# Retention rope: rotating by a matmul instead of a stream shuffle, with moved weight splits and one bank less

## The reference

```
q = xpos_rotary(q, pos)
k = xpos_rotary(k, pos) * d ** -0.5

def rotate_every_two(x):
    x1, x2 = x[..., ::2], x[..., 1::2]
    return stack((-x2, x1), axis=-1).reshape(x.shape)

def xpos_rotary(x, pos):
    return x * cos(phase) + rotate_every_two(x) * sin(phase)
```

## Time and profile before

| what | value |
|---|---|
| median of 3 runs | 1906.66 us (1906.11 to 1907.75) |
| profiled execution | 1907.75 us, its span 1906.0 us |
| TensorE busy | 98% of the span |
| TensorE weight loads | 80% |
| VectorE busy | 64% |
| ScalarE busy | 42% |
| mean granted TensorE clock | 0.996 of full |
| DMA, mean | 84 GB/s |
| TensorE in the chain that ended last | 94% |

### The profile page before, as it was taken

One profiled execution on the slowest core, in us unless ns is written; L12 is line 12 of the kernel. 1 busy time (PEld: TensorE's weight loads), 2 busy tenths in 40 slices (PEclk: granted clock), 3 DMA queues, 4 the chain that ended last, 5 costly groups with the idle time before them and its releaser, 6 DMA issues.

```text
span 1906.0 us, 21837 instructions
## 1 busy us (share of the span) xinstructions
PE 1867.9 (98%) x8604; PEld 1517.2 (80%) x8604; DVE 1227.9 (64%) x1764; ACT 797.6 (42%) x1286; POOL 0.2 (0%) x4
## 2 busy tenths in 40 slices
PE   8999999999999999999999999999999899999999
PEld 6766889788888888766788888887888688888887
DVE  5865865667777434676767777336888667777521
ACT  4237411544444333355644444325665544444311
POOL 0000000000000000000000000000000000000000
PEclk9999999999999999999999999999999999999999
DMA  6211100232232233211333322322111033223232
GB/s 230 96 59 55 56 23 7 81 113 91 97 100 97 91 99 101 87 34 34 111 100 99 99 91 93 102 92 79 65 45 45 24 110 100 93 95 100 91 100 75
DMA packets 48646, 160.13 MB, mean 84 GB/s; under 512 B 5528, under 2 KB 6040, under 8 KB 48416
## 3 DMA queue, kind: packets, MB, share of 16 engines
q1 hardware_dynamic: 48544, 158.74, 25.6%
HBM read 156.62 MB, written 2.10 MB: 83 GB/s over the span
## 4 chain that ended last, share of the span: by engine, by line
PE 94%; ACT 3%; DVE 2%; issue 1%; DMA 0%; SPq 0%; ACTq 0%; DVEq 0%
PE bank L166 93%; DVE mixer_arena L1059 1%; ACT mixer_arena L647 1%; ACT wh L647 1%; PE bank L535 0%; DVE mixer_arena L1067 0%; ACT L647 0%; DVE wl L1059 0%; ACT conf_diag_l L647 0%; ACT conf_diag_h L647 0%; DMA raw<-in_w_in 0%; ACT even_arena L647 0%; DVE sq L1059 0%; PE bank L368 0%; DVE even_arena L1556 0%
## 5 line engine op out<-in xcount | busy, mean ns | idle before, releaser
L647 ACT ACTIVATE wh<-raw 128x1024 fp32r<-128x1024 f32 (+2 forms) x310 | 308.8, 998 | 735.4 <-PE bank L166 726.0
L166 PE MATMUL bank<-nh,wh 128*128 128x512 f32 x1520 | 600.5, 395 | 8.3 <-DVE nl L1067 8.3
L166 PE MATMUL bank<-nl,wh 128*128 128x512 f32 x1520 | 593.0, 390 | 0.0
L166 PE MATMUL bank<-nh,wl 128*128 128x512 f32 x1520 | 592.9, 390 | 0.0
L1059 DVE TENSOR_TENSOR wl<-raw,wh 128x1024 fp32r<-128x1024 f32 (+2 forms) x310 | 355.8, 1148 | 247.2 <-ACT wh L647 246.3
L166 PEld LDWEIGHTS bank<-nh,wh 128*128 128x128 f32 x1520 | 286.3, 188 | 74.4 <-DVE wl L1059 8.9
L166 PEld LDWEIGHTS bank<-nl,wh 128*128 128x128 f32 x1520 | 286.2, 188 | 61.1 <-issue 2.6
L166 PEld LDWEIGHTS bank<-nh,wl 128*128 128x128 f32 x1520 | 286.2, 188 | 60.1
L166 PE MATMUL bank<-ff_yh,wh 128*128 128x512 f32 x528 | 205.4, 389 | 0.0
L166 PE MATMUL bank<-ff_yl,wh 128*128 128x512 f32 x528 | 205.4, 389 | 0.0
L166 PE MATMUL bank<-ff_yh,wl 128*128 128x512 f32 x528 | 205.4, 389 | 0.0
(11 more groups left out here) (193 smaller groups left out, 1784.9 us busy)
## 6 DMA issues: line engine op xcount, KB each, us to landing
raw<-in_ff_a_up SPq DMA_DIRECT2D x44, 512.0 KB, 3.2
raw<-in_ff_b_up SPq DMA_DIRECT2D x44, 512.0 KB, 3.3
raw<-in_ff_c_up SPq DMA_DIRECT2D x44, 512.0 KB, 3.2
raw<-in_w_in SPq DMA_DIRECT2D x32, 512.0 KB, 3.3
raw<-in_pw SPq DMA_DIRECT2D x24, 512.0 KB, 3.3
raw<-in_even_in SPq DMA_DIRECT2D x16, 512.0 KB, 3.2
raw<-in_ff_a_down_a SPq DMA_DIRECT2D x8, 512.0 KB, 3.2
raw<-in_ff_a_down_b SPq DMA_DIRECT2D x8, 512.0 KB, 3.2
```

The source lines that it names most:

```text
L166: return e.matmul(out, lhsT, rhs, start=start, stop=stop, skip_group_check=True)
L647: return e.activation(out, in_, func, **kw).then_inc(n.give(sem), 1)
```

## The change

The neighbour swap of each rope becomes a f32 matmul with a constant 128x128 matrix `rotate` (entries 1 and -1, so the sin table loses its signs). `swap(s)` on TensorE writes bank 4 + s % 2, and VectorE's sin product reads that bank. The rotations stand behind pieces 3 to 7 (s = 0 to 4), behind piece 8 (s = 5 and 6) and behind the first token piece (s = 7). Rope 4 moves before the gates' scaling. A load for `rotate` goes between those of the tables and `select`. The GDN's piece i = 0 uses bank 0 instead of 6. VectorE scales the token blocks after the last `feed()` of the token pieces. The first `feed()` of the gate pieces moves on ScalarE behind the three silus, and on VectorE before the eight head scalings.

```diff
+    def swap(s):
+        e.wait_ge(c.evac, s + 1)
+        if s >= 2:
+            e.wait_ge(c.rope_done, s - 1)
+        x = (m1.rq if s < HEADS else m1.rk)[:, s % HEADS, :]
+        mm(bank[4 + s % 2][:, :], m1.rotate, x, True, True).then_inc(n.give(c.swap_done), 1)
...
             root_columns(6)
+            e.wait_ge(c.mix_ready, 16 * 3)
+        if s >= 3:
+            swap(s - 3)
     take(0)
     piece(0, c.nh, c.nl, range(DK))
-    e.wait_ge(c.mix_ready, 16 * 2)
-    token_pieces()
+    swap(5)
+    swap(6)
+    token_pieces(between={0: (7,)}, fn=swap)
...
     for i in range(12):
-        j = i % 2 if i else 6
-        take(j)
-        piece(j, c.nh, c.nl, range(DK))
+        take(i % 2)
+        piece(i % 2, c.nh, c.nl, range(DK))
...
         if i == 1:
-            vacate(6)
...
     roots_of(8, 4, 1.0)
-    feed()
     for q in (9, 10, 11):
         silu(q)
     for i in range(9):
         if i < 8:
-            if i:
-                feed()
+            feed()
             group()
...
     def rope(s):
         x = (m1.rq if s < HEADS else m1.rk)[:, s % HEADS, :]
         e.wait_ge(c.evac, s + 1)
-        settle()
-        e.stream_shuffle(m1.ropes[2 + s % 2], x, [i ^ 1 for i in range(32)]).then_inc(n.give(c.vec_step), 1)
         tt(m1.ropes[s % 2], x, m1.cos, ALU.mult, c.vec_step)
-        settle()
-        tt(m1.ropes[2 + s % 2], m1.ropes[2 + s % 2], m1.sin, ALU.mult, c.vec_step)
+        e.wait_ge(c.swap_done, s + 1)
+        tt(m1.ropes[2 + s % 2], bank[4 + s % 2][:, :], m1.sin, ALU.mult, c.vec_step)
         settle()
         tt(x, m1.ropes[s % 2], m1.ropes[2 + s % 2], ALU.add, c.rope_done)
...
         if s >= 4:
             rope(s - 4)
+    rope(4)
     z, az, ln = m1.z[0:64, :], m1.az[0:64, :], m1.ln[0:64, :]
     arrive()
     tt(z, bank[0][0:64, :], c.r[0:64, :], ALU.mult, c.evac)
     feed()
-    rope(4)
...
     for w in range(RING):
         arrive()
-        if w == RING - 1:
-            e.wait_ge(c.rcol_ready, 1)
-            for t in range(TB):
-                ts(m1.rv[:, t, :], bank[t][:, :], c.rcol[:, t:t + 1], ALU.mult, c.evac)
         feed()
...
+    e.wait_ge(c.rcol_ready, 1)
+    for t in range(TB):
+        ts(m1.rv[:, t, :], bank[t][:, :], c.rcol[:, t:t + 1], ALU.mult, c.evac)
...
-            if i == 0:
-                for q in range(4, 12):
-                    head_scale(q)
-                settle()
             feed()
+        if i == 0:
+            for q in range(4, 12):
+                head_scale(q)
+            settle()
...
             load(m1.tables, d["tables"], c.mix_ready)
+            load(m1.rotate, d["rotate"], c.mix_ready)
             load(m1.select, d["select"], c.mix_ready)
```

More of the change, by code:

```diff
@@ L118 @@
  tap_done conv_done silu_done glu_done ah_ready al_ready
- ea_ready gates_for_act gates_logged rope_done
+ ea_ready gates_for_act gates_logged swap_done rope_done
  ret_scored ret_weighed ret_done ret_copied decay_rows gcols_done gcols_ready spread spread_taken spread_used dec_ready decayed
@@ L1269, in vector_program @@
             e.wait_ge(c.gdn_conv, i - 2)
-        scaled(m1.pad[:, i % 3, TAPS_GDN - 1:TAPS_GDN - 1 + S], i % 2 if i else 6)
+        scaled(m1.pad[:, i % 3, TAPS_GDN - 1:TAPS_GDN - 1 + S], i % 2)
         feed()
@@ L1812, in build @@
             tables=A[:, 43 * S:45 * S], cos=slots(A, 43), sin=slots(A, 44), z=slots(A, 45), az=slots(A, 46), ln=slots(A, 47),
-            select=slots(A, 42),
+            rotate=A[:, 49 * S:49 * S + P], select=slots(A, 42),
             rows=slots(A, 22), d=c.sq[:, 0, :].rearrange("p (t s) -> p t s", s=P),
@@ L1882, in shape_constants @@
     out = dict(consts=np.concatenate([np.ones((P, P)), np.eye(P)], 1))
+    rotate = np.zeros((P, P))
+    rotate[i[1::2], i[0::2]] = -1.0
+    rotate[i[0::2], i[1::2]] = 1.0
+    out["rotate"] = rotate
     out["select"] = np.concatenate([np.repeat((i == h)[:, None] * 1.0, P, 1) for h in range(HEADS)], 1)
@@ L1897, in shape_constants @@
     phase = (np.arange(S, dtype=np.float32)[None, :] * np.repeat(angle, 2).astype(np.float32)[:, None]).astype(np.float64)
-    out["tables"] = np.concatenate([np.cos(phase), np.where(i % 2, 1.0, -1.0)[:, None] * np.sin(phase)], 1)
+    out["tables"] = np.concatenate([np.cos(phase), np.sin(phase)], 1)
     rel = np.arange(S)[None, :] - i[:, None]
```

## The result

| | before | after |
|---|---|---|
| median of 4 executions | 1907.2 us (1906.11 to 1907.75) | 1928.03 us (1927.16 to 1929.57) |
| profiled execution, its span | 1907.75, 1906.0 us | 1928.18, 1926.4 us |
| mean granted clock | 0.996 | 0.994 |

The ratio is 1.0111, 95% interval 1.0093 to 1.0129: the change makes the kernel 20.8 us slower; the spans differ by 20.4 us.

The account below looks back on a forecast made before the run. TensorE, busy 98% of the span, was taken to bound the kernel. The terms 6.9 - 1.0 + 3.3 + 5.55 + 1.7 + 2.1 = 18.5 us, on the median 1906.66, gave 1925.2 us, range 1919 to 1930.

Parts of the forecast that it names:

- eight rotations less the gate piece's wait: On TensorE, eight f32 products at 0.86 us add 6.9 us; the wait between gate and token pieces goes, saving 1.0.
- bank 0 behind copy and split: After the last token piece, TensorE waits 3.3 us because VectorE scales the values only after the weight copy and split.
- head scalings behind copy and split: Before the first chunk transposes, TensorE goes on 5.55 us later, as the head scalings follow the late copy and split.
- clock behind the first wait: Behind the new 3.3 us wait, the granted clock falls to half, costing 1.7 us; bounds 0 and 2.6.
- clock behind the second wait: Behind the 5.8 us wait, the granted clock falls to half, costing 2.1 us; bounds 0 and 2.6.
- the old fall at 164 us goes: The clock fall traced near 163 us; the prediction said only that an old fall may go, with nothing in the sum.
- The slack of 0.7 us for rotation 6: Rope 4 ends near 63.2, rotation 6 needs it at 63.9, so it does not wait; the smallest margin.
- the 2.38 us: Time from a piece's arrival to the end of VectorE's weight split, by piece 7's pattern, used for the bank 0 wait.
- Rival (b): Weight copies are ready at both moved splits, so the waits are 1.0 and 1.25 us: 8.1 in all, 1914.8; chance 0.07.
- Rival (c): After the late head scalings, TensorE waits for the banks again, about 5.5 us more, 1931 us; chance 0.08.
- Rival (d): VectorE held TensorE, so its relief recovers 6.8 us and neither moved split costs a wait: +0.1, 1906.8; chance 0.05.
- rival (a): The clock does not fall at one or both new waits, or an old fall goes: about 1922.4 us; chance 0.22.

Follow-up runs that it names:

- rotations_alone: The kernel before with only the eight rotations, their table load and the earlier rope 4: ratio 1.0037, 7.1 us slower.
- bank_and_order_alone: The kernel before with bank 0 for the GDN's first piece and the values scaled behind the weight split: ratio 1.0025, 4.8 us slower.
- both_splits_again: The kernel before with ScalarE's copy behind the three silus and VectorE's split ahead of the eight head scalings, rerun on another chip: ratio 1.0051.
- bank_alone: The kernel before with only bank 0 for the GDN's first piece, values still scaled ahead of the split: ratio 1.0003.
- vector_split_alone: The kernel before with only VectorE's split moved ahead of the eight head scalings, ScalarE's copy where it was: ratio 1.0015.
- fewer_waits: The kernel before with its gate piece in bank 4 and part of ScalarE's exponentials, and VectorE's use of them, a turn later: ratio 0.9996.
- both_splits_moved: The kernel before with ScalarE's copy behind the three silus and VectorE's split ahead of the eight head scalings, first run: ratio 1.0057, 10.9 us slower.
- filled_waits: The changed kernel with unread matmuls in its two new TensorE waits: ratio 1.0087 to the kernel before, against 1.0111 for the changed kernel.
- the two filled versions of before: The kernel before with unread matmuls in six TensorE waits, without and with the gate piece in bank 4: ratios 0.9974 and 0.9975.

## Why the prediction was right

The forecast was 1925.2 us, range 1919 to 1930; measured 1928.0. The sum was 18.5 us on top of the profiled execution, and the spans differ by 20.4.

| term | forecast | measured | where |
|---|---|---|---|
| eight rotations less the gate piece's wait | 6.9 - 1.0 | 6.0 | B - A, rotations_alone |
| bank 0 behind copy and split | 3.3 | 3.35 | B - A, bank_and_order_alone |
| head scalings behind copy and split | 5.55 | 5.5 | C - B, both_splits_again; wait 5.79 in after |
| clock behind the first wait | 1.7 | 1.7 | 3.4 us at half clock |
| clock behind the second wait | 2.1 | 2.5 | C to the next transposes, 10.7 against 8.2 |
| the old fall at 164 us goes | 0 | -1.0 | C - B: 119.39 against 118.34 to 118.39 where it did not come |
| a fall at 915 us | 0 | +1.7 | 4 us at 0.57 |

These sum to 19.8 us. The rest is 0.3 us by which the changed kernel's execution was late already at mark A, and some tenths at the end. The mechanisms of the first five rows all came as forecast, at their places and within half a microsecond of their sizes: the queue order of `feed()` on the two elementwise engines decided both waits. The slack of 0.7 us for rotation 6 held: TensorE has no idle time there. One reading was loose without harm: the 2.38 us that it counts from the piece's arrival to the end of the split run from the start of VectorE's scaling, 0.2 us later, and the sum adds that 0.20 itself. Rival (b), copies that are not in the way, is refuted by bank_alone beside bank_and_order_alone. Its price of the second wait had an error of its own: I had put the split alone at 1.2 us, but vector_split_alone shows 2.54, since VectorE must wait for the copy even where ScalarE does it early, and a fall came behind that wait too. Rival (c) fell: no second wait for VectorE followed, the later waits kept their lengths. Rival (d) fell with rotations_alone. Of rival (a) only the part about an old fall came true.

The mis-sized term is the clock away from the edits. I priced the falls at the two new waits and only mentioned that old ones may go. In fact the profiled execution of the changed kernel lacks one old fall (164 us) and has another that before lacks (915 us). That these two nearly cancel, -1.0 and +1.7, is luck; no run shows that the change caused either of them, and the two runs of both splits show that one and the same code can have its falls at different places. The old fall was worth 1.0 us and not the 1.7 that its 3.4 us at half clock suggest, because without it TensorE waits for ScalarE's roots instead, here in the changed kernel:

```profile
201.75 1.53 PE L166 MATMUL bank<-mixer_arena,consts 128*128 128x512 f32 x3 [0.59 <-ACT mixer_arena L656]
```

Before, this wait does not exist. The wait of 0.6 us stands in all profiles that have no fall at the wait of 2.35 us, and in none that has it.

The prediction read from one profile that three of three waits above 2.2 us had a fall. Over all profiles this was too sure for the shorter ones. The wait of 2.35 us had a fall in five of the profiles of the table (before, rotations_alone, both runs of both splits, vector_split_alone) and none in five others that have the wait unfilled; that of 2.21 us (1328 us) had one in seven of eleven. For the longer ones it held: 2.79, 3.2, 5.8 and 5.9 us had a fall each time, in 1, 2, 3 and 11 unfilled cases. The wait of 2.16 us in fewer_waits had none. The Trainium skill (TensorE: Matmul & The Clock Gate, part on the HAM clock gate) says that the monitor behind the clock runs free of the kernel. The changing counts at one and the same wait fit this; no run shows the monitor itself.

## What to carry to other kernels

In this kernel, where one engine is busy 98% of the time, each operation moved onto it cost its whole duration, and the ones taken from an engine that idles there brought nothing; a bank number alone removed the wait that two rotations were put into. In an engine that runs its program in order, a pipeline step set in front of an evacuation passes on everything that it waits for itself: 1.0 us became 3.3, and 0.25 became 5.8. Look up for such a step what releases it on the other engine before placing it.

## What the runs showed of the hardware that was not expected

- The clock fell behind waits well below 2 us too, but not always: behind a pair of waits of 1.5 and 1.4 us at 131 to 139 us in four of the eleven profiles that leave them unfilled (rotations_alone, bank_alone, both_splits_moved, filled_waits), behind 1.3 and 1.1 us between 893 and 915 us in six of thirteen (after, both_splits_again, vector_split_alone, filled_waits and the two filled versions of before). In the other profiles it stayed at 1.00 at the same places. A fall of 3.4 us at half clock costs up to 1.7 us, one of twice that length up to 3.4. Such falls, here or there, are enough for the time of one kernel to spread by several us, and the mean clocks of single executions above fit that.
- Unread matmuls in a wait kept the clock up behind it and were free here, where they end before the wait does: some 3.4 to 4.6 us off the changed kernel (with the reservation above), 4 to 5 us off the kernel before (0.9974, interval 0.9964 to 0.9984).
- Mark A, before any edit, lies between 32.9 and 35.6 us in the table. Two kernels are better compared from such a mark than from the start.
